# The second scan of a two-block network laid out anew: 128 rows of keys and values, four quarters of the array for the triangular inverse

## The reference

```python
def rwkv7_scan(r, w, k, v, a_vec, b_vec):          # each (1, 1024, 8, 64)
    def step(state, inp):                          # state (1, 8, 64, 64)
        r_t, w_t, k_t, v_t, a_t, b_t = inp
        sa = jnp.einsum('bhvk,bhk->bhv', state, a_t)
        state = (state * w_t[:, :, None, :] + sa[..., None] * b_t[:, :, None, :]
                 + v_t[..., None] * k_t[:, :, None, :])
        y_t = jnp.einsum('bhvk,bhk->bhv', state, r_t)
        return state, y_t
    s0 = jnp.zeros((B, H, N, N), jnp.float32)
    _, y = lax.scan(step, s0, xs)
```

## Time and profile before

| what | value |
|---|---|
| median of 3 runs | 2667.02 us (2664.51 to 2668.92) |
| the profiled execution's own time | 2663.65 us |
| its span (first to last instruction) | 2661.9 us |
| TensorE, its weight loads | 2513.4 us (94%), 2052.1 us (77%) |
| DVE, ACT, POOL | 1420.5, 848.4, 937.6 us |
| first of `chunk_products` in pairs 0 to 7 | 2203.6, 2230.9, 2261.1, 2291.3, 2323.3, 2352.7, 2382.0, 2411.4 us |
| first of `read_state(14)`, the tail's start | 2440.1 us |
| last DVE operation of the scan starts | 2448.28 us |

### The profile page before, as it was taken

How to read it: one execution, slowest core, us unless ns; L and a number is a source line. 1 busy time by engine, 2 the same in 40 slices (tenths; PEclk the granted TensorE clock), 3 DMA queues, 4 the chain that set the end, 5 groups by cost and what they waited for, 6 DMA issues and landing times. The chain is left out here.

```text
span 2661.9 us, 40568 instructions
## 1 busy us (share of the span) xinstructions
PE 2513.4 (94%) x17201; PEld 2052.1 (77%) x17201; DVE 1420.5 (53%) x2047; ACT 848.4 (32%) x1393; POOL 937.6 (35%) x489
## 2 busy tenths in 40 slices
PE   7998999999999999998989889999998998899997
PEld 5887778888888888886867558778776778887786
DVE  6112543253352221223387599999984664566844
ACT  3214553321120110223342354543515541212231
POOL 3212424443342332444443216435523201111674
PEclk9999999999999999999999999999999999999998
DMA  3113313122222111112224203224233002101523
GB/s 132 48 41 103 103 32 111 48 83 83 84 83 83 60 48 48 48 48 87 64 87 167 64 18 133 82 99 137 76 107 119 25 17 82 35 4 68 181 72 111
DMA packets 82084, 207.67 MB, mean 78 GB/s; under 512 B 8392, under 2 KB 21744, under 8 KB 81904
## 3 DMA queue, kind: packets, MB, share of 16 engines
q1 hardware_dynamic: 74992, 192.48, 21.9%
q10 hardware_dynamic: 6912, 12.59, 1.3%
HBM read 170.81 MB, written 35.27 MB: 77 GB/s over the span
## 5 line engine op out<-in xcount | busy, mean ns | idle before, releaser
L332 PE MATMUL ps<-region_rounded,weights_hi_by_slot 128*128 128x512 f32 x2432 | 962.7, 396 | 38.2 <-DVE region_rounded L610 14.2
L334 PE MATMUL ps<-region_rounded,weights_lo_in_place 128*128 128x512 f32 x2432 | 952.0, 391 | 0.0
L333 PE MATMUL ps<-region_rounded,weights_hi_by_slot 128*128 128x512 f32 x2432 | 951.6, 391 | 0.0
L326 POOL TENSOR_TENSOR weights_lo_in_place<-wbuf,weights_hi_by_slot 128x1024 fp32r<-128x1024 f32 x194 | 485.2, 2505 | 718.9 <-ACT weights_hi_by_slot L322 718.8
L332 PEld LDWEIGHTS ps<-region_rounded,weights_hi_by_slot 128*128 128x128 f32 x2432 | 460.6, 189 | 146.1 <-issue 42.5
L333 PEld LDWEIGHTS ps<-region_rounded,weights_hi_by_slot 128*128 128x128 f32 x2432 | 460.6, 189 | 98.6 <-issue 3.8
L334 PEld LDWEIGHTS ps<-region_rounded,weights_lo_in_place 128*128 128x128 f32 x2432 | 459.7, 189 | 96.9
L322 ACT CAST weights_hi_by_slot<-wbuf 128x1024 fp32r<-128x1024 f32 x194 | 201.7, 1043 | 349.9 <-DMA wbuf<-w_mlp 218.9
L2048 DVE MAX8 gcols<-region 128x8 f32<-128x384 f32 (+5 forms) x192 | 171.6, 893 | 6.1
L2050 DVE MATCH_REPLACE8 region<-gcols,region 128x384 f32<-128x384 f32 (+5 forms) x192 | 168.2, 876 | 0.0
L1353 POOL TENSOR_TENSOR region_rounded<-region,region_rounded 128x512 fp32r<-128x512 f32 x64 | 83.0, 1298 | 215.2 <-DVE region_rounded L1494 215.2
(11 more groups left out here) (331 smaller groups left out, 3435.3 us busy)
## 6 DMA issues: line engine op xcount, KB each, us to landing
wbuf<-w_mlp SPq DMA_DIRECT2D x64, 512.0 KB, 3.6
wbuf<-w_hn SPq DMA_DIRECT2D x37, 512.0 KB, 3.8
wbuf<-w_in SPq DMA_DIRECT2D x25, 512.0 KB, 3.7
region<-xT SPq DMA_DIRECT2D x24, 512.0 KB, 6.7
xtra<-w_ada SPq DMA_DIRECT2D x32, 384.0 KB, 4.2
scratch_hn_out<-tmp ACTq DMA_DIRECT2D x48, 256.0 KB, 2.7
region<-scratch_hn_out SPq DMA_DIRECT2D x24, 512.0 KB, 8.6
wbuf<-w_att SPq DMA_DIRECT2D x20, 512.0 KB, 3.6
```

What stands on the lines that cost most here:

```text
L326: self.nc.gpsimd.tensor_tensor(self.m.lo4[:, n % SLOTS, :], self.m.raw4[:, n % SLOTS, :], self.m.hi4[:, n % SLOTS, :].bitcast(F32), ALU.su ...
L332: nc.tensor.matmul(out, m.hi4[:, s, w], m.rounded(hi + k, half(hf)), start=(k == 0), stop=False)
L333: nc.tensor.matmul(out, m.hi4[:, s, w], m.rounded(lo + k, half(hf)), start=False, stop=False)
L334: return nc.tensor.matmul(out, m.lo4[:, s, w], m.rounded(hi + k, half(hf)), start=False, stop=(k == KT - 1))
```

## The change

All of it is in `rwkv_scan`. What lies in which rows and banks is different, and the semaphores with it; the arithmetic is the same, and so is the order of the steps on TensorE.

- Masked products: `mb` and `mk` become one `mats_s`. For chunk `par`, b's products lie in the rows of `par` and k's in the other 64 rows, in the same columns. In the same way u lies in the rows of `par` and v in the other 64, over the place of v (even chunks) or a (odd chunks); and the turned keys of b and k over the place of b (even) or k (odd).
- `use_u`: one product over all 128 rows where there were two over 64 that were summed.
- `turn`: b and k by 16 products of K = 128 with 64 weight columns against the identity, a and v by 32 small ones, where there were 16 transposes. ACT has five copies where it had four, and waits for b and k together and for a and v together.
- The transposed inverse `invt` and `y1s` have the rows of the other chunk for heads with `hh` = 1. The two halves of a step are now `hh` 0 and `hh` 1. "T" of `hh` 1 writes its two results to two banks, and its products go to all four quarters; so do `level0`, `g` and `uv`. `wt` did so before.
- POOL: four multiplies over 64 rows each, chained one behind the other, and an add; level 0 waits for the multiplies and no longer for the add, which is in front of the first "T". DVE adds the identity in `first_inverse`, where it copied.
- Banks: the pair of banks for chunk 0 and 1 alternates with `i`, so the first half of `chunk_products` waits for `wt_copied` and the second for `uv_copied`. The output of `use_u` goes to the second half of bank 6; `read_state` waits for `y_added` before its second half only.
- `add_u`: one operation over both heads for two.

```diff
             def chunk_products(i):
-                if i:
-                    pe.wait_ge(uv_copied, 2 * i)
-                    pe.wait_ge(wt_copied, 2 * i)
-                for q, g in enumerate((RB, RK)):
+                for par in range(2):
+                    if i:
+                        pe.wait_ge([wt_copied, uv_copied][par], 2 * i)
+                    cols = chunk_cols(2 * i + par)
                     for p in range(RP):
-                        for par in range(2):
+                        for q, g in enumerate((RB, RK)):
                             for hh in range(2):
-                                last = nc.tensor.matmul(m.ps[tile64(par), 2 * q + hh, p * P:(p + 1) * P],
+                                last = nc.tensor.matmul(m.ps[tile64(par ^ q), banks(i)[par] + hh, p * P:(p + 1) * P],
                                                         m.chunk(g + p, cols, rows=tile64(hh)),
                                                         m.ra[tile64(hh), :, p, cols], start=True, stop=True)
                     last.then_inc(mats, 2)
             def turn(i):
-                for q, g in enumerate((RB, RK, RA, RV)):
-                    pe.wait_ge(mats_masked, 4 * i + q + 1)
+                for par in range(2):
+                    pe.wait_ge(mats_masked, 4 * i + par + 1)
                     for p in range(RP):
-                        last = nc.tensor.transpose(m.ps[:, q, p * P:(p + 1) * P],
-                                                   m.chunk(g + p, slice(i * P, (i + 1) * P)), m.const("ident"))
+                        for q, g in enumerate((RB, RK)):
+                            last = nc.tensor.matmul(m.ps[tile64(par ^ q), A + par, p * P:(p + 1) * P],
+                                                    m.chunk(g + p, chunk_cols(2 * i + par)), m.const("ident"),
+                                                    start=True, stop=True)
                     last.then_inc(turned, 1)
+                pe.wait_ge(mats_masked, 4 * i + 4)
+                for g, at in ((RA, 0), (RV, 256)):
+                    for p, par in groups:
+                        for hh in range(2):
+                            o = tile64(par ^ hh if g == RA else 1 - par)
+                            last = nc.tensor.matmul(m.ps[o, B + hh, at + p * RL:at + (p + 1) * RL],
+                                                    m.chunk(g + p, chunk_cols(2 * i + par), rows=tile64(hh)),
+                                                    eye[tile64(hh)], start=True, stop=True)
+                    last.then_inc(turned, 1)
             def level0(i):
-                pe.wait_ge(first_level, i + 1)
+                pe.wait_ge(first_cols, 4 * i + 4)
+                pe.wait_ge(tok_copied, 5 * i + 2)
...
             def level(i, l):
...
+                for hh in range(2):
+                    pe.wait_ge(y1_masked, n + hh + 1)
...
+                    for p in range(RP):
+                        for q in (1, 0) if l < LEVELS - 1 else (1,):
+                            for par in range(2):
+                                o = tile64(par ^ hh)
+                                a, b = ((invt, y1s), (y1s, invt))[q]
+                                bank, at = grown_bank(i, l, hh, q)
+                                last = nc.tensor.matmul(m.ps[tile64(par) if q == 0 else o, bank, at + p * RL:at + (p + 1) * RL],
+                                                        hx(a, p, hh)[o], hx(b, p, hh)[o], start=True, stop=True)
                     last.then_inc(ty, 1)
             def read_state(c):
                 if c:
                     pe.wait_ge(s_scaled, c)
-                    pe.wait_ge(y_added, c)
...
                 if c:
-                    pe.wait_ge(rs_copied, c)
+                    pe.wait_ge(y_added, c)
             def use_u(c):
-                pe.wait_ge(u_added, 2 * c + 2)
+                pe.wait_ge(u_added, c + 1)
                 for p in range(RP):
                     for hh in range(2):
-                        out = m.ps[tile64(hh), 7, p * 64:(p + 1) * 64]
-                        nc.tensor.matmul(out, by_token(RB, i, r, p, hh), hx(u, p, hh)[r], start=True, stop=False)
-                        last = nc.tensor.matmul(out, by_token(RK, i, r, p, hh), by_token(RV, i, r, p, hh),
-                                                start=False, stop=True)
+                        last = nc.tensor.matmul(m.ps[tile64(hh), 7, p * 64:(p + 1) * 64], keys(c, p, hh), values(c, p, hh),
+                                                start=True, stop=True)
                 last.then_inc(s_ready, 1)
+                pe.wait_ge(rs_copied, c + 1)
...
+                        last = nc.tensor.matmul(m.ps[tile64(hh), 6, 256 + p * 64:256 + (p + 1) * 64], values(c, p, hh),
+                                                mats_s[:, c // 2 % 2, c % 2, hh, p, 0:64], start=True, stop=True)
                 last.then_inc(y_ready, 1)
         def _(pool):
-                pool.wait_ge(mats_masked, 4 * i + 2)
-                for hh in range(2):
-                    nc.gpsimd.tensor_tensor(heads(invt)[:, :, hh, :], mb[:, i % 2, hh, :, 64:128], lv, ALU.mult
-                                            ).then_inc(first_cols, 1)
...
+                for n, (par, hh) in enumerate(((0, 0), (0, 1), (1, 0), (1, 1))):
+                    r = tile64(par)
+                    if n:
+                        pool.wait_ge(first_cols, 4 * i + n)
+                    pool.wait_ge(mats_masked, 4 * i + n + 1)
+                    nc.gpsimd.tensor_tensor(heads(x0)[tile64(par ^ hh), hh], mats_s[r, i % 2, par, hh, :, 64:128], lv[r],
+                                            ALU.mult).then_inc(first_cols, 1)
         def _(act):
-                for q, g in enumerate((RB, RK, RA, RV)):
-                    act.wait_ge(turned, 4 * i + q + 1)
-                    nc.scalar.copy(m.chunk(g, slice(i * P, (i + 1) * P), n=RP), by_pair(m.ps[:, q, :])).then_inc(tok_copied, 1)
+                act.wait_ge(turned, 4 * i + 2)
+                for par in range(2):
+                    nc.scalar.copy(m.chunk((RB, RK)[par], slice(i * P, (i + 1) * P), n=RP), by_pair(m.ps[:, A + par, :])
+                                   ).then_inc(tok_copied, 1)
+                act.wait_ge(turned, 4 * i + 4)
+                nc.scalar.copy(ra_tok.rearrange("p (b x) -> p b x", b=2), m.ps[:, B:B + 2, 0:256]).then_inc(tok_copied, 1)
+                for par in range(2):
+                    k = tile64(1 - par)
+                    nc.scalar.copy(all_values(2 * i + par, k), by_head(m.ps[k, B:B + 2, 256:512])).then_inc(tok_copied, 1)
```

More of the change, by code:

```diff
@@ L2319, in heads, with cell, keys, values @@
     def heads(ap):
-        return ap.rearrange("p (a b c) -> p a b c", a=RP, b=2)
+        return ap.rearrange("p (b a c) -> p b a c", a=RP, b=2)
     def hx(ap, p, hh):
-        return heads(ap)[:, p, hh, :]
-    def by_token(g, i, r, p, hh):
-        return m.chunk(g + p, slice(i * P + 64 * hh, i * P + 64 * hh + 64), rows=r)
+        return heads(ap)[:, hh, p, :]
+    def cell(p):
+        return slice(p * RL, p * RL + RL)
+    def keys(c, p, hh):
+        return m.chunk((RB, RK)[c % 2] + p, slice(c // 2 * P + 64 * hh, c // 2 * P + 64 * hh + 64))
+    def values(c, p, hh, rows=slice(None)):
+        return m.chunk((RV, RA)[c % 2] + p, slice(c // 2 * P + 64 * hh, c // 2 * P + 64 * hh + 64), rows=rows)
+    def all_values(c, rows):
+        return m.chunk((RV, RA)[c % 2], slice(c // 2 * P, c // 2 * P + P), rows=rows, n=RP).rearrange(
+            "r a (b x) -> r b a x", b=2)
+    def banks(i):
+        return 2 * (i % 2), 2 - 2 * (i % 2)
+    def rows_bank(i, hh):
+        return abs(3 * (i % 2) - hh)
     def chunk_cols(c):
         return slice(RL * c, RL * c + RL)
[L2332 to L2337, removed]
+    groups = [(p, par) for p in range(RP) for par in range(2)]
     z_loaded, gb_loaded, attn_gated, attn_hi, attn_lo = S("attn_z_loaded"), S("gb_loaded"), S("attn_gated"), S("attn_hi"), S("attn_lo")
@@ new lines, in level0, with grown_bank, level @@
+                last.then_inc(y1, 2)
+            def grown_bank(i, l, hh, q):
+                if hh == 0:
+                    return 3 - rows_bank(i, 0), 256 * q
+                return (1 + q if l < LEVELS - 1 else 3 - rows_bank(i, 1)), 0
+            def level(i, l):
+                n = 2 * (GROWS * i + l - 1)
+                for hh in range(2):
+                    if l == 1:
+                        pe.wait_ge(first_rows, 2 * i + hh + 1)
+                    else:
+                        pe.wait_ge(t_grown, n - 2 + hh + 1)
+                    for p, par in groups:
+                        r = tile64(par)
+                        last = nc.tensor.matmul(m.ps[tile64(par ^ hh), rows_bank(i, hh), cell(p)],
+                                                mats_s[r, i % 2, par, hh, p, 64:128], hx(inv, p, hh)[r],
@@ L2420, in apply_inverse @@
+                last.then_inc(g_ready, 2)
                 pe.wait_ge(t_grown, 2 * GROWS * (i + 1))
@@ L2589, in add_u @@
```

(2 more changed lines are left out.)

120 lines of the change are left out of this document (54 added, 66 removed).

## The result

| | before | after |
|---|---|---|
| median of 4 runs each | 2666.91 us (2664.51 to 2668.92) | 2648.84 us (2647.15 to 2650.28) |
| the profiled execution's own time, its span | 2663.65, 2661.9 us | 2650.12, 2648.3 us |
| TensorE, its weight loads, POOL busy | see the table of before | 2496.5, 2026.8, 950.4 us |

The ratio is 0.993, with a 95% interval of 0.9917 to 0.9942: 18.1 us less. The forecast was 2646.7, with 20.3 us saved.

What follows compares the result with a forecast made beforehand. TensorE was taken as nearly the bound, but not alone, with waits for ACT, POOL and DVE. Savings of 18.4 us in the pairs and 1.9 in the tail, 20.3 in all, gave a median of 2646.7 us, range 2638 to 2660.

Steps and rivals of the forecast that it cites:

- pair 0: First pair of chunks, without read_state or use_u: level 0 late by 0.6, four levels give 0.84, the end 1.75; saves 2.0.
- Steps 1, 2 and 4: Start of a pair: first products unchanged at 1.80 us; turning 1.0 us more; level 0 at 6.07 (before 5.37).
- rival B: TensorE's 128x64 tiles don't run side by side, so turning and use_u take longer: 2666 us, no change; chance 11%.
- Step 3: POOL's four chained multiplies over 64 rows: 0.73 + 0.05 us each, costing nothing up to about 1.0 us each.
- Rival C: Level 0 waits for POOL's four chained multiplies, which use up the gain from 1.6 us each; up to 2690 us; chance 5%.
- Step 5: First use_u drops from 1.86 to 0.94 us, hidden behind five DVE operations 0.46 apart; level 1's mask at 9.11 (before 8.90).
- Step 6: Inverse levels: second head's T four-wide, 0.48 us; a level becomes a 3.13 loop through the first head, shorter by 0.21.
- the tail: Bare chain after the eight pairs: shorter use_u and output halves, read_state no longer waiting for the output sum; saves 1.9 us.
- Step 7: End of a pair: g, wt and u products 0.48 us each; next pair starts after wt's copies at 26.94, before 29.36.
- The cast's 0.6: Pairs 0 to 3, with ACT's 1.06 cast queued: u's copies end at 28.4, second half of first products 0.6 us late.
- rival D: Small costs (shape changes of 0.3, another stall or two, POOL at 1.2), 1 us a pair: 2655 us; chance 10%.

Runs made afterwards that it cites:

- first experiment: The changed kernel with POOL's large operation of each pair made to wait for DVE's scaling of the state in that pair: 2641.54 us, ratio 0.9916.
- third experiment: The changed kernel with a pair's first products waiting at their start for both wt's and u's copies, as before the change: 2655.84 us, ratio 0.9965.

## Why the prediction was right, point by point

The number was near, and in part by luck: pair 0 cost 3.0 us and pairs 5 to 7 1.1 us more than forecast, pairs 1 to 4 gave 2.5 more, and the sum of 20.3 came out as 18.75.

**Steps 1, 2 and 4** held: level 0 is at 6.11 behind ACT's copy (forecast 6.07), and 128x64 tiles do run side by side, which was the open question behind rival B.

**Step 3** held: 0.79 each against 0.78, and nobody waits. Rival C needed 1.0. But POOL did cost something by another way, which no step had: the chain of multiplies ends later, the large operation behind it now lies over DVE's scaling, and without that a pair that follows no cast is 0.8 to 1.0 shorter (first experiment).

**Step 5**: the row of five at 0.46, 2.30 in all, gave T1 at 9.58; it is at 9.79. Two errors of opposite sign: from 2380.85 to the mask at 2383.31 it is 2.46, of which the scaling's hold is 0.67; the rest, 1.79, is 0.5 less than forecast.

**Step 6**: T1 to T2 was forecast at 3.54 and is 3.72, T2 to T3 at 4.24 and is 3.99; a level at 3.13 is 3.14 or 3.15. The loop through the first head sets it, as forecast: another order shortened just that loop and the level fell to 2.67. I ascribed the gain of a level over before to the four-wide second half. That is open: with 0.3 of its 0.46 us taken back, the level keeps 3.15. That the two halves now lie on different quarters, so that T need not queue behind L's last records, would do it as well, and no run separates the two. The largest single part of the gain is the second use_u: T2 to T3 was 4.93 before, is 3.99 now and 4.77 with doubled products. So 0.78 of the 0.94 is use_u's, the rest the level's; for seven pairs that is 5.5 us, with 1.1 in the tail (8.08 against 7.00) 6.6 of the 18.75. Step 5 had the first use_u hidden behind DVE. That holds only in the pairs where POOL holds DVE up; in pairs 1, 2 and 4 undoing it cost 0.68 each. Undoing both cost 12.0 in all, with the stalls that came.

**Step 7**: the next pair at 27.06 against 26.94, right behind wt's copies (2401.00) and ahead of the end of u's (2401.70). The cast's 0.6 was right: level 0 is at 6.69 in pairs 1 to 4 and at 6.06 in pair 5, and with POOL out of the way the pairs differ by it (26.97 and 26.34). That pairs 1, 2 and 4 last 27.13 and not 27.55 comes from DVE's row, 0.5 too long in the forecast, and from T2 to T3, 0.25 too long, less 0.16 of POOL's hold and 0.18 from T1 to T2. In pairs 5 to 7 the same errors are eaten up by POOL's hold of 0.7 to 0.9, which no term had. The third experiment puts 0.6 to 0.7 a pair on the split wait; its 7.6 in all holds the clock and the scaling as well.

**Pair 0** is the largest miss, 28.24 for 25.3. The sum left one stall of issue where it had been, in pair 3, and took none elsewhere. Such a stall was named in rival D, not in the forecast's sum, and it cost 3.0 us: 1.70 of stall and some 1.2 of the low clock behind it. The prediction left the clock out, on a busy share of near 80% to come; TensorE was busy for 90%, and the clock fell all the same where TensorE had stood. Pairs 1 to 4 saved 2.5 more than forecast, pairs 5 to 7 1.1 less, and the tail 0.05 less.

## What to carry over

When a change makes an engine off the path finish later, look at what that engine does next and which instructions of others it will now lie over, even where no semaphore joins them. In a loop of latencies, the order of the same products and smaller additions for what is waited for first (9.1 us) were worth half as much as the whole new layout. A saved product counts only where no other engine is the later one at that place: of two equal use_u the second cost 0.8 of its 0.94 in the pairs without new stalls, the first 0.7 where DVE was free and nothing where POOL held DVE up. And before a total is read, the pairs that the edit cannot have touched are worth a look: pair 0's stall moved the scan by up to 2.3 us in runs that had nothing to do with it.

## What the runs showed of the hardware

- **POOL holds up DVE.** A DVE operation with both inputs in SBUF, 128x256 fp32, took 0.42 alone and 1.09 to 1.32 when it began under POOL's 2.37 us operation; it ended 0.3 after POOL did (2382.77 and 2383.06). Those with one input in PSUM kept 0.41 in the same place. The Trainium skill (GPSIMD Engine Reference, "Specifications") says that the two share their SBUF interfaces and names DVE instructions with two SBUF inputs among those that contend; the trace agrees.
- **Instructions are fetched by DMA and can come late.** Packets of the queue "instruction", pair 4 and on after the change, 25 us:

```profile
DMA packets 6, 0.10 MB, mean 4 GB/s; under 512 B 0, under 2 KB 0, under 8 KB 0
...
q8 instruction: 6, 0.10, 1.5%
```

Six of 16 KB in 25 us, one in 4.2. Under loads at 387 GB/s TensorE stood for 1.70 us, and the granted clock behind it was 0.53 for 3 us. The Trainium skill (Runtime: NRT & Kernel Launch, "Instruction fetch mechanics") says that instructions arrive in lines of 16 KB, read ahead, and that this stays hidden because an engine issues more slowly than they arrive. The packets' size agrees; that the fetch stays hidden does not hold here, with 3.1 us of stalls in this scan and up to 6.1 in the denser kernels. That these stalls are late packets rests on their going away with the loads and on the packet that came 6.25 us behind the one before it; the short ones of the densest kernels weren't taken apart.
- **The granted clock can fall behind a stretch in which TensorE stood**, from 2.4 GHz to near 1.2: to 0.50 from 2223.3 to 2226.6 after a stall of 1.70, for 3.4 us behind the 2.5 us stall of the first experiment, and from 2229 to 2232 behind a wait of 1.64 in the third. 64 records of first products took 3.61 then and 1.98 at full clock. Behind pair 3's stall of 1.12 it stayed.
- **Tiles run ahead of each other** by 0.1 to 0.17 us: in pair 6 after, line 2483 has its first record at 2385.47, where line 2476, ahead of it in the program, still starts one at 2385.64. That their quarters are free at that moment is how the lines' tiles lie, not something that a record shows.
